# Moving four vector-engine steps of a conditioning matvec from the attention output projection to the start of the MLP loop

## Reference

```python
cond = jax.nn.silu(c)
for i in range(2):
    mod = cond @ w_ada[i] + b_ada[i]          # [1024] @ [1024, 6144]
    sh1, sc1, g1, sh2, sc2, g2 = jnp.split(mod, 6, axis=-1)
    h = rms_norm(x, ln_mix_g[i]) * (1.0 + sc1) + sh1
    y = nsa_mixer(h, ...) if i == 0 else diff_mixer(h, ...)   # ends in  o @ w_out
    x = x + g1 * y
    h = rms_norm(x, ln_mlp_g[i]) * (1.0 + sc2) + sh2
    x = x + g2 * (jnp.square(jax.nn.relu(h @ w_mlp_in[i])) @ w_mlp_out[i])
```

## Time and profile before

| | |
|---|---|
| median of 3 runs | 1516.41 us (1512.63 to 1519.85) |
| the profiled execution | 1516.41 us |
| its span, first to last instruction | 1514.7 us |
| mean granted PE clock | 0.970 |
| PE / PEld / DVE / ACT / POOL busy | 96% / 90% / 64% / 41% / 4% |
| moved by DMA | 260.94 MB, mean 172 GB/s |

### The profile page before, as it was taken

How to read it: one execution, slowest core, us unless ns; L and a number is a source line. 1 busy time by engine, 2 the same in 40 slices (tenths; PEclk the granted TensorE clock), 3 DMA queues, 4 the chain that set the end, 5 groups by cost and what they waited for, 6 DMA issues and landing times.

```text
span 1514.7 us, 26270 instructions
## 1 busy us (share of the span) xinstructions
PE 1447.9 (96%) x11023; PEld 1365.9 (90%) x11023; DVE 964.2 (64%) x1205; ACT 628.4 (41%) x793; POOL 65.9 (4%) x111
## 2 busy tenths in 40 slices
PE   7999999999999999989999899999989998999998
PEld 6999999889999999988986578999979876899998
DVE  5679877545677767766415866788874476555453
ACT  5444454444433343444522644334444325344441
POOL 4030000000000000000000000000000000000000
PEclk9999999999999999999976999999999989999999
DMA  8555543433587887854510025889963420256551
GB/s 234 190 181 194 164 142 125 156 123 126 196 275 260 277 276 256 268 177 118 188 56 0 1 89 177 292 293 322 315 206 112 153 84 1 84 169 192 180 180 56
DMA packets 173573, 260.94 MB, mean 172 GB/s; under 512 B 5509, under 2 KB 148146, under 8 KB 173362
## 3 DMA queue, kind: packets, MB, share of 16 engines
q1 hardware_dynamic: 160890, 203.13, 41.4%
q0 software_dynamic: 10128, 51.30, 10.0%
q10 hardware_dynamic: 2472, 5.31, 1.2%
HBM read 258.67 MB, written 1.05 MB: 171 GB/s over the span
## 4 chain that ended last, share of the span: by engine, by line
PE 78%; DVE 12%; ACT 4%; DMA 3%; issue 2%; SPq 1%; ACTq 0%; DVEq 0%
PE ring L635 59%; PE acc L635 18%; DVE w_lo L1661 2%; ACT w_hi L1209 2%; DMA raw<-in_w_mlp_in_dram 1%; DVE arena L1707 1%; ACT arena L1209 1%; DMA raw<-in_w_in_dram 1%; DVE arena L1799 1%; PE acc L1045 1%; DVE h_lo L1701 1%; DVE norm L1676 1%; DMA raw<-in_diff_w_in_dram 1%; DVE arena L2182 1%; DVE arena L2179 0%
## 5 line engine op out<-in xcount | busy, mean ns | idle before, releaser
L1661 DVE TENSOR_TENSOR w_lo<-raw,w_hi 128x2048 fp32r<-128x2048 f32 (+1 forms) x191 | 437.0, 2289 | 340.5 <-ACT w_hi L1209 340.2
L635 PE MATMUL ring<-h_hi,w_hi 128*128 128x256 f32 x2088 | 597.9, 286 | 10.9 <-DVE h_lo L1701 7.3
L635 PE MATMUL ring<-h_lo,w_hi 128*128 128x256 f32 x2088 | 592.0, 284 | 0.0
L635 PE MATMUL ring<-h_hi,w_lo 128*128 128x256 f32 x2088 | 591.9, 283 | 0.0
L1209 ACT ACTIVATE w_hi<-raw 128x2048 fp32r<-128x2048 f32 (+1 forms) x191 | 363.7, 1904 | 244.5 <-DMA raw<-in_w_mlp_out_dram 70.6
L635 PEld LDWEIGHTS ring<-h_hi,w_hi 128*128 128x128 f32 x2088 | 402.0, 193 | 18.7 <-DVE h_lo L1701 7.1
L635 PEld LDWEIGHTS ring<-h_lo,w_hi 128*128 128x128 f32 x2088 | 402.1, 193 | 0.4
L635 PEld LDWEIGHTS ring<-h_hi,w_lo 128*128 128x128 f32 x2088 | 401.8, 192 | 0.0
L635 PE MATMUL acc<-e_hi,w_hi 128*128 128x256 f32 x768 | 218.6, 285 | 0.1
L635 PE MATMUL acc<-e_hi,w_lo 128*128 128x256 f32 x768 | 217.3, 283 | 0.0
L635 PE MATMUL acc<-e_lo,w_hi 128*128 128x256 f32 x768 | 217.3, 283 | 0.0
(11 more groups left out here) (261 smaller groups left out, 1358.3 us busy)
## 6 DMA issues: line engine op xcount, KB each, us to landing
arena<-in_w_ada_dram POOLq DMA_DIRECT2D x64, 768.0 KB, 5.9
raw<-in_w_mlp_in_dram SPq DMA_DIRECT2D x32, 1024.0 KB, 5.5
raw<-in_w_mlp_out_dram SPq DMA_DIRECT2D x32, 1024.0 KB, 5.1
raw<-in_w_in_dram SPq DMA_DIRECT2D x24, 1024.0 KB, 5.2
raw<-in_w_e_gate_dram SPq DMA_DIRECT2D x16, 1024.0 KB, 5.6
raw<-in_w_e_up_dram SPq DMA_DIRECT2D x16, 1024.0 KB, 6.4
raw<-in_w_e_down_dram SPq DMA_DIRECT2D x16, 1024.0 KB, 6.4
raw<-in_diff_w_in_dram SPq DMA_DIRECT2D x12, 1024.0 KB, 5.1
```

The source lines that it names most:

```text
L635: return nc.tensor.matmul(dst, lhs, rhs, start=start, stop=stop, **kw)
L1661: tt(w_lo[q % SPL][:, 0:n], raw[q % RAW][:, 0:n], w_hi[q % SPL][:, 0:n].bitcast(F32), ALU.subtract)\
```

## The change

`residual` loses its `behind` callback (a `last_sem` argument takes its place in the signature and is not used), so DVE's steps for pieces 0 to 3 no longer stand between the four additions of n_o. `pieces(0)`, which did nothing, now does all four of them. It is called after `chunk_lo(0)` and before the loop. The steps for pieces 4 to 31 stay where they are.

```diff
-            def residual(name, scale=None, behind=None):
+            def residual(name, scale=None, last_sem=None):
...
-                    if behind is not None and i < 3:
-                        behind(i)
...
-            def first_pieces(i):
-                for n in ((0,), (1, 2), (3,))[i]:
-                    ada(1, n)
-
-            residual("n_o", scale=lambda b: mods[:, 0, 16 + b:17 + b], behind=first_pieces)
+            residual("n_o", scale=lambda b: mods[:, 0, 16 + b:17 + b])
...
-                    if l == 0 and c and ADA_FIRST + 2 * c - 2 < 2 * STEPS:
+                    if l == 0 and c == 0:
+                        for n in range(ADA_FIRST):
+                            ada(1, n)
+                    elif l == 0 and ADA_FIRST + 2 * c - 2 < 2 * STEPS:
                         ada(1, ADA_FIRST + 2 * c - 2)
                         ada(1, ADA_FIRST + 2 * c - 1)
```

## The result

The kernel after took 1527.1 us (median of 9, 1520.26 to 1531.88), the kernel before 1516.41 (median of 9, 1512.63 to 1519.85). The ratio is 1.0063, 95% interval [1.0046, 1.0081]: about 9.6 us slower, where 5.3 had been forecast. One execution each of two later kernels, `pair_early` (1992 us) and `unrolled` (1993 us), fell into a slow state and stands in no median, mean or ratio here.

What follows compares the result with a forecast made beforehand. PE, busy for 96% of the span, was taken as the bound, so only its waits count. 0 from n_o plus 5.3 us at the second group of transposes, on 1516.4, gave 1521.7 us; range 1514 to 1529.

Steps and rivals of the forecast that it cites:

- n_o gives: Removing four piece steps, 6.5 us of DVE, from n_o gains nothing, at most 0.1 us, because PE is full there.
- `w_lo` of panel 5: Early in mlp0, this DVE step starts at 950.9 instead of 943.55 us, behind pieces 2 and 3.
- first stall: Early in mlp0, PE waits 2.0 us for `e_lo` of chunk 1 before the `down` of panel 4.
- transfer of panel 7: In mlp0, this weight transfer, with two piece loads beside it, takes 7.0 us (5.5 to 8.0).
- PE late at the first group: PE's first group of transposes in mlp0, waiting for piece 7, starts 5.8 us late (5.1 to 6.8).
- The landing wait: At the start of mlp0, DVE idles about 4 us before piece 2, whose load goes out only once piece 0 is used.
- The transfers as the bound: Rival: mlp0 has no room for the moved 3.1 MB of loads, so 9.8 us longer, 1526.2 us; chance 0.17.
- The second group: PE's second group of transposes in mlp0 is 5.3 us late net (4.8 to 7.7), taking 8.49 us for a long transfer.
- the prediction's own term for PE: At the second group of transposes, PE by itself is 4.8 us late: 5.8 less the 1.04 us idle before.
- The clock: Rival: a PE stall in mlp0 drops the clock to half for up to 6.8 us, costing 3.4, 1525.1 us; chance 0.08.
- a clock below 1.00 between 950 and 980: Sign named beforehand as proving the forecast wrong: PE's granted clock falls in this stretch (us) of mlp0.
- the rest of the program is shifted as it is: Last step: behind the second group of transposes, DVE is no later than PE and nothing more is lost.

Runs made afterwards that it cites:

- pair_early: The kernel before with every pair of pieces from 4 on used one loop step earlier, pieces 0 to 3 left in n_o: 1517.64 us, ratio 1.0019.
- unrolled: The kernel after with PE's loop of mlp0 written out, same instructions in the same order: 1526.5 us, ratio 1.0070 against before.
- after, again: The kernel after, unchanged, measured and profiled a second time: 1525.36 us, ratio 1.0054 against before.
- half: The kernel before with only the steps of pieces 2 and 3 moved to the start of mlp0, pieces 0 and 1 left in n_o: 1517.8 us, ratio 0.9994.
- short_after: The kernel after with DVE's steps for pieces 0 to 3 cut to 8 of 1536 columns, loads whole: 1524.27 us, ratio 1.0045 against before.
- no_load23: The kernel after without layer 1's loads of pieces 2 and 3, whose steps read the buffers of pieces 0 and 1: 1522.67 us, ratio 1.0056 against before.
- low_between: The kernel after with `w_lo` of panel 5 run between pieces 1 and 2: 1526.79 us, ratio 1.0076 against before.
- delay_only: The kernel before, all pieces left in n_o, with 15 unused multiplications (about 10.7 us) on DVE behind `e_lo` of chunk 0: 1520.74 us, ratio 1.0022.
- short_fill: The kernel `unrolled` with 4 idle PE matmuls before the `down` of panel 4 and 7 before the first transposes: 1527.09 us, ratio 1.0061 against before.
- unrolled again: The kernel `unrolled`, unchanged, measured and profiled a second time: 1528.55 us, ratio 1.0065 against before.

## Why the prediction was right and where it was wrong

The direction and the path were right. Counted from the start of the stage, forecast and profile after:

| step | forecast | after | after, again |
|---|---|---|---|
| n_o gives | 0 | 0 (19.00 us both) | |
| DVE idle before piece 2 | about 4 | 4.13 | |
| `w_lo` of panel 5 | 24.7 | 24.7 | |
| first stall | 2.0 | 2.14 | 2.31 |
| transfer of panel 7 | 7.0 (5.5 to 8.0) | 7.8 | 7.0 |
| PE late at the first group | 5.8 (5.1 to 6.8) | 6.5 | 5.9 |
| wait at the second group | close to none | 0 | 0 |
| PE late at the end of the stage | 5.3 | 6.8 | 4.7 |
| whole program, by the ratio | 5.3 | 9.6 | 8.2 |

- **The landing wait** came where it was put and with its size. `half` (no wait, no loss) shows that the steps which start the chain of loads are the ones that cost. `short_after` (wait without work, 5.0 late) and `no_load23` (work without wait, 2.2 late) make the wait the main part at the first group, in one profile each; their times, 1.0045 and 1.0056, do not confirm it.
- **The first stall** was right in size but is not a loss by itself, as `low_between` shows. The sum took the total at the first group, so that was counted rightly.
- **The transfers as the bound** (+9.8) came near the measured number, for another reason. That rival wanted a loss that grows from group to group. It is 6.5, 6.9 and 6.8 us in after; the steady part carries 305 GB/s at a share of 0.92, less than before (320 at 0.96), and no later group waits. Loads moved by about 40 us found room. What the Trainium skill, "DMA: Bandwidth & Descriptors", section "Issuing engines are not separate DMA queues", says of loads from two queues, that they interleave on the same engines, agrees with panel 7: 7.80 us with piece loads beside it, 5.3 without (`delay_only`). Here that was worth some 2 us on one transfer, which the forecast had in its 7.0.
- **The second group** was mis-sized: 5.3 us net. The chain over two weight transfers, from which the 5.3 came, did not repeat; PE's own time set it. That is 6.5 - 1.04 = 5.5, and the clock's 7.07 - 5.76 = 1.3 makes 6.8, where the profile shows 6.9. So the 5.3 lies near the measured stage by luck: the prediction's own term for PE, 4.8, was the one that applied, 0.7 too small, and the clock was missing from it.
- **The clock** was a rival at 0.08 with 3.4 us, and nothing of it stood in the sum. It did fall, behind waits of 4 us and also of 2.3 us, though for 3.4 us in each of the two profiles of after and not 6.8, so the price there is 1.3 or nothing. The text asked for "a clock below 1.00 between 950 and 980" as a sign against the forecast, and that is what came. The Trainium skill, "TensorE: Matmul & The Clock Gate", section "Why this matters for your kernels", warns of such gaps; the traces agree in kind, by the 0.50 and 0.51 windows above, but not every such gap did it: the clock stayed up at the 2.14 us of after.

**What was missing.** Over all runs compared, 31 of after and 105 of before, the means are 1525.8 ± 0.7 and 1516.6 ± 0.3 us: 9.1 us (1525.78 - 1516.65). From the last addition of n_o to the first addition of the MLP, the two profiles of before measure 202.7 and 201.9 us, two of after and two of the unrolled ones 209.2, 207.1, 209.7 and 207.2. So 6.0 of the 9.1 us lie in that stretch. n_o and the 8.2 us from its last addition to the first matmul of mlp0 measure the same in all of these. The rest of the program scatters more than what is sought: from the first addition of the MLP to the end it takes 394.0 and 396.9 us in before and 393.5 to 396.6 in the others, and up to the first addition of n_o, where the change has no part, 899.0 and 903.0 in before and 895.1 to 899.5 in the others. And three of the four profiled executions of after and unrolled (1521.0, 1519.7 and 1520.2 us) lie 4.8 to 6.1 us under their kernels' means. The other 3 us are placed by no profile: they may lie outside the stage, or in the stage in executions that were not profiled. The mean granted clock goes with them: 0.9664 after, 0.9679 before, that is 1525.8 x 0.0336 - 1516.6 x 0.0321 = 2.6 us more of lost speed, an estimate; the fall inside the stage, 3.4 us at half speed, is already 1.7 us of it. The profiled execution of after had 0.968, one of its better ones. `no_load23` points the same way: 1.0 us lost in the stage's profile, mean clock 0.9650, ratio 1.0056. The kernels that use pieces 0 and 1 in mlp0 have a mean clock of 0.9646 to 0.9673, those that use them in n_o one of 0.9664 to 0.9682. The two sets overlap. Where in the program the clock is lower, and whether it is cause or companion, stays open; fillers in the two waits of mlp0 did not bring it back (0.9664 with `short_fill`).

So in the stage the profiles give 6.0 us against 5.3, a small miss, and some 3 us more are in the times that no step of the prediction had. The weak step is the last one, "the rest of the program is shifted as it is", if these 3 us lie outside the stage; that was not shown.

## What to carry to other kernels

When a step that consumes a buffer is moved, the load that waits for this buffer moves with it. Before pricing the step's own time, ask when the next load can then go out and what stands behind the consumer in its queue while it lands: here, in single profiles at the first group, 6.5 us of work cost 1.2 us and the landing waits about 5; the program's times are too coarse to confirm this split. Ask too which transfer the moved loads will run beside: one weight transfer took 2 us longer. If steps have to move, move those whose data is already there and leave the ones that start the chain of loads, as `half` did at no measurable cost.

## What the runs showed of the hardware

- A granted clock of 0.50 for 3.4 us followed a PE wait of only 2.31 us (after again), of 2.11 us (unrolled again) and of 2.48 us (delay_only), but not waits of 2.14 us (after), 2.04 us (unrolled), 2.05 us (no_load23) and 2.00 us (unrolled again, the second). Around the waits of 4.15 us (short_after) and 4.91 us (low_between) it was low for 6.8 us. One execution doesn't tell whether a wait of 2 us costs its clock.
- The fall ahead of another wait cost nothing (after again), the one behind the last wait did (after): 1.3 us for 3.4 us of half speed, since 48 matmuls took 7.07 us instead of 5.76.
- A weight panel of 1 MB landed 5.3 to 5.5 us after its issue at this place (before, delay_only) and 7.0 to 8.1 us where piece loads ran beside it for most of that time (both profiles of after, half, short_after).
- A piece of 768 KB landed 5.7 us after its issue with weight panels beside it, and 4.6 to 6.4 us shortly afterwards, the same as in n_o. Their transfer times gained nothing from being moved out of n_o.
